# Expert units of a two-layer encoder: token rows fetched by an indirect transfer and turned on TensorE, and the last gated block turned inside the down product ahead of it

## The chip, the cores and the metric

The kernel runs on one core of a Trainium2 chip, as one program with one launch. The metric is the device time in microseconds (us) of an execution; lower is better.

## What is computed

The reference is an encoder trunk for 256 tokens of width 1024 in float32. Layer 0 is a neighbourhood attention beside a memory attention, and a dense SwiGLU. Layer 1 is a gated linear attention beside a memory attention, and a mixture of experts. Only the mixture matters here:

```python
def moe_swiglu(x, w_router, w_gate, w_up, w_down):   # x: the normalised tokens
    logits = xf @ w_router                           # 8 experts
    top_val, top_idx = lax.top_k(logits, 2)
    weights = jax.nn.softmax(top_val)
    # per expert e, for the tokens that chose it:
    #   y = (silu(x @ w_gate[e]) * (x @ w_up[e])) @ w_down[e]     w_gate, w_up 1024x3584, w_down 3584x1024
    # and h += weight * y for each token
```

Each expert holds 44 MB of weights, all eight are read once.

## The kernel before, in words

**Products in three parts.** Every weight block is split into a high part (rounded to the fast float32r type by ScalarE, `w_hi`) and a low part (the difference, by VectorE, `w_lo`), and so is the left operand. A product is then three matmuls, `w_hi*x_hi`, `w_lo*x_hi`, `w_hi*x_lo` (`mul3`, L1356 to L1360). A weight block of 128x2048 values (1 MB) is called a slot; three slots of `w_hi` and `w_lo` exist (CUT = 3), so the high part of slot j can be made only when TensorE has finished slot j-3 (`slot_done`). SyncE issues the loads, about ten slots ahead (`expert_loads`, L445 to L470), each one when the low part of the slot that lay in its place has been made.

**Units.** The mixture is worked off in units of up to 128 tokens of one expert. There are eight experts and up to three further units where an expert has more than 128 tokens; in the execution profiled there are eight units. All engines run the same loop over the units (`Fori`), each with its own body and semaphores between them. A unit has 42 slots: for c = 0 to 6 a gate product (2 slots), an up product (2 slots) and a down product (2 slots) over a block of 512 of the 3584 hidden columns. One slot is 12 matmuls with 512 columns.

**Order on TensorE in a unit** (L1884 to L1914): `hidden("gate", c)`, then `turn_hidden(c-1)` (four 128x128 transposes of the gated block of c-1, L1867), `hidden("up", c)`, `down(c-1)`. After c = 6: `turn_hidden(6)`, `gather(u+1, 0)`, `down(6)`, `gather(u+1, 1)`, and the scatter (L1911), eight matmuls. `gather(v, b)` (L1832 to L1838) forms half of the next unit's left operand, already turned: four output blocks of 128x128, each as two matmuls of `xn` (all 256 tokens) with the 0/1 matrix `pick` (256x128), which says which token stands in which place of the unit. The result is in PSUM bank 2+b; ScalarE copies it to `gx_hi` (`gather_high`, L744) and VectorE makes `gx_lo` (`gather_low`, L1258).

**Order on ScalarE** (L777 to L806): the high parts (L767), for each c silu (L787) and `hT_high(c-1)` (L780), and at the end of a unit the high part of slot 41, `hT_high(6)`, the high part of slot 42 (slot 0 of the next unit), `gather_high(u+1, 0)`, the high part of slot 43, the two halves of `y_hi` (L804) and `gather_high(u+1, 1)`.

**Order on VectorE** (L1320 to L1350): for each c the low parts (L1306) up to three slots ahead of the product, `hT_low(c-1)` (L1317), and after the low part of the slot three behind the up product the gated block `hid` (L1327), silu times up. `build_picks(u+1)` (L1255) follows `hid` of c = 5. At the end of a unit: the low part of slot 41, `hT_low(6)`, slot 42, `gather_low(u+1, 0)`, the two halves of `y_lo` (L1339), slot 43, `gather_low(u+1, 1)`, and two weighted additions to `h` (L1349). The low part of slot 44, the first of the next up product, comes after these.

**GpSimd** has only small operations, for the norms (`inverse_root`, L824 and L827) and in the linear attention (L845, L847), and nothing in the unit loop.

Of the kernel before, what the change touches and what calls it, by code (L numbers as in the profile page):

```python
# [18 lines left out]
ALU = mybir.AluOpType  # L19
ACT = mybir.ActivationFunctionType  # L20
F32 = mybir.dt.float32
F32R = mybir.dt.float32r
I32 = mybir.dt.int32
AX_X = mybir.AxisListType.X

# [103 lines left out]
def shape_constants(np):  # L129
# [7 lines left out]
    def put(name, a):  # L137
        full = np.zeros((P, a.shape[1]), np.float32)
        full[: a.shape[0]] = a
        col[name] = (sum(x.shape[1] for x in parts), a.shape[1])  # L140
        parts.append(full)
# [10 lines left out]
    put("ones", np.ones((P, P)))  # L152
    put("iota", np.broadcast_to(np.arange(P), (P, P)))
    x, dc = np.arange(SHIFT_W)[None, :], np.arange(RPB_C)[:, None]
    shifts = np.zeros((2, 2, 32, SHIFT_W), np.float32)
# [14 lines left out]
def build(nc, col, tables, shifts, x, mem, gains, rpb, gate_aug, g_norm, router, mem_kv, even_in, even_out,  # L170
          even_gate, even_up, even_down, odd_in, odd_out, exp_gate, exp_up, exp_down, out):
    with ExitStack() as ctx:
        def sb(name, shape, dt=F32):
            return ctx.enter_context(nc.sbuf_tensor(name, shape, dt))
# [28 lines left out]
        rt_lo = sb("rt_lo", [P, KD, E], F32R)  # L203
        unit_i = sb("unit_i", [P, 4], I32)
        states = sb("states", [P, 2, 3, DV])
        ARENA = 13464
# [68 lines left out]
        unit_f = take(4)  # L275
        r_at = top[0]
        gx_hi, gx_lo = xt_hi[:, :, 0:P], xt_lo[:, :, 0:P]
        y_hi, y_lo = xt_hi[:, :, P:T], xt_lo[:, :, P:T]
# [50 lines left out]
        def STATE_PS(d, k):  # L329
# [48 lines left out]
        y_half, y_hi_ready, y_lo_ready, scattered = (  # L378
            sem("y_half"), sem("y_hi_ready"), sem("y_lo_ready"), sem("scattered"))
        h_added = [sem(f"h_added_{t}") for t in range(TT)]  # L380

# [109 lines left out]
        def _(act):  # L491
# [262 lines left out]
            with act.Fori(0, n_more + E) as u:  # L754
# [28 lines left out]
                for c in range(NC):  # L783
# [6 lines left out]
                    if c == 4:  # L790
                        act.wait_ge(pick_turned, u + 1)
                        act.activation(pickT[:].rearrange("p t s -> p (t s)"), ps[:, 7, 0:2 * P],
                                       ACT.Copy).then_inc(pickT_ready, 1)
                high_unit(UNIT_SLOTS - 1)
                hT_high(NC - 1)
# [18 lines left out]
        def _(pool):  # L814
# [27 lines left out]
            for i in range(GH):  # L842
# [4 lines left out]
                pool.tensor_tensor(gss[:, 2, k], gss[:, 1, k], mhalf[:, 0:TT], ALU.pow).then_inc(o_rstd, 1)  # L847
            inverse_root(4, BY_HALF)
            inverse_root(5, BY_TOKEN)


        @block.vector
        def _(dve):
# [442 lines left out]
            with dve.Fori(0, n_more + E) as u:  # L1296
# [24 lines left out]
                for c in range(NC):  # L1321
                    if c >= 1:
                        low_unit(moe_slot("gate", c, 1) + CUT)
                        hT_low(c - 1)
                    unit_products(moe_slot("up", c, 1))
                    dve.wait_ge(silu_ready, u * NC + (c + 1))
                    dve.tensor_tensor(hid[:, c % 2, :], silu_sb[:, c % 2, :], ps[:, 2 * (c % 2) + 1, :],  # L1327
                                      ALU.mult).then_inc(hid_ready, 1)
                    if c == 5:
                        dve.wait_ge(pick_turned, u + 1)  # L1330
                        build_picks(u + 1)
                low_unit(UNIT_SLOTS - 1)
                hT_low(NC - 1)
# [21 lines left out]
        def _(pe):  # L1355
# [489 lines left out]
            with pe.Fori(0, n_more + E) as u:  # L1845
# [23 lines left out]

                def down(i):  # L1870
                    pe.wait_ge(hT_lo_ready, u * NC + (i + 1))
                    for half in range(2):
                        w = cut_slot(moe_slot("down", i, half), 2)
                        for n in range(2):
# [5 lines left out]
                            if i == NC - 1 and half == 1 and n == 0:  # L1880
                                ins.then_inc(y_half, 1)
                        ins.then_inc(slot_done, 1)

                for c in range(NC):  # L1884
# [10 lines left out]
                    hidden("up", c)  # L1895
                    if c >= 1:
                        down(c - 1)
                    if c == 3:
                        for t in range(TT):
                            ins = pe.transpose(ps[:, 7, P * t:P * (t + 1)], pick[:, t, :], ident)  # L1900
                        ins.then_inc(pick_turned, 1)
                turn_hidden(NC - 1)
                gather(u + 1, 0)
                down(NC - 1)
                gather(u + 1, 1)

# [50 lines left out]
```

## Time and profile before

| | |
|---|---|
| median of three runs | 1506.14 us (1502.95 to 1506.96) |
| the profiled execution: its own time | 1505.14 us |
| the profiled execution: span of the core | 1503.3 us |
| TensorE matmuls (PE) busy | 1457.3 us, 97% |
| TensorE weight loads (PEld) busy | 1240.3 us, 83% |
| VectorE (DVE) busy | 1170.6 us, 78% |
| ScalarE (ACT) busy | 978.4 us, 65% |
| GpSimd (POOL) busy | 21.4 us, 1% |
| DMA | 428.42 MB, mean 285 GB/s |
| mean granted TensorE clock | 0.985 of full speed |

The units fill the span from 499.3 us to the end. The profile gives for each group of instructions its busy time and what ended the idle time before it; the trace gives each instruction's start and duration. A matmul with 512 columns is shown with a duration of 0.39 us, but matmuls are pipelined: what counts is the distance from one start to the next. "PE" is the matmul, "PEld" the load of its stationary operand, which can run ahead of it. A float32 matmul of `gather` has two entries in the trace, so its eight matmuls are shown as x16; a transpose and a float32r matmul have one. The granted clock is given as a share of 2.4 GHz: 1.00 or 0.50.

### The profile page before, as it was taken

How to read it: one execution, taken by the hardware profiler on the slowest of the kernel's cores; microseconds unless marked ns; L12 is line 12 of the kernel's file. 1: busy time of each engine (PE TensorE's matmuls, PEld its weight loads, DVE VectorE, ACT ScalarE, POOL GpSimd, SP SyncE). 2: the span in 40 equal slices, each digit the busy share in tenths (PEclk: the TensorE clock that was granted, in tenths of full speed). 3: DMA queues.
4: the chain of work that ended last, by engine and by line, in shares of the span. 5: the costliest groups of instructions: out<-in, count | busy, mean ns of one | idle time of the engine just before them, and what ended most of it. 6: DMA issues, size and time to landing. Idle time of an engine off the chain costs nothing.

```text
span 1503.3 us, 20846 instructions
## 1 busy us (share of the span) xinstructions
PE 1457.3 (97%) x7832; PEld 1240.3 (83%) x7832; DVE 1170.6 (78%) x986; ACT 978.4 (65%) x904; POOL 21.4 (1%) x41
## 2 busy tenths in 40 slices
PE   6999999999998899999999999999999999999997
PEld 6986999998966788888888888888888888888885
DVE  5667544544774798898888888888888888898887
ACT  5455444334833677777777777777777777777775
POOL 1000000000010000000000000000000000000000
PEclk9999999999998999999999999999999999999999
DMA  9534555535535599899999989989989998998982
GB/s 320 192 115 137 186 194 183 181 115 162 161 113 196 183 387 369 317 376 376 324 344 385 376 302 383 374 310 372 378 308 369 383 365 312 375 369 319 372 323 90
DMA packets 198192, 428.42 MB, mean 285 GB/s; under 512 B 8805, under 2 KB 39041, under 8 KB 198146
## 3 DMA queue, kind: packets, MB, share of 16 engines
q1 hardware_dynamic: 198146, 427.79, 79.3%
q8 instruction: 30, 0.49, 0.1%
q14 instruction: 16, 0.13, 0.0%
HBM read 426.71 MB, written 1.05 MB: 285 GB/s over the span
## 4 chain that ended last, share of the span: by engine, by line
PE 88%; DVE 5%; ACT 3%; issue 2%; DMA 1%; POOL 0%; SPq 0%; DVEq 0%; POOLq 0%; ACTq 0%
PE ps L1358 27%; PE ps L1360 27%; PE ps L1359 27%; PE ps L1867 1%; DVE w_lo L1306 1%; PE ps L1836 1%; ACT w_hi L767 1%; PE ps L1911 1%; DVE w_lo L871 1%; ACT w_hi L505 1%; DMA raw<-mem_kv 1%; PE ps L1482 0%; PE ps L1804 0%; PE ps L1446 0%; PE ps L1379 0%
## 5 line engine op out<-in xcount | busy, mean ns | idle before, releaser
L1306 DVE TENSOR_TENSOR w_lo<-raw,w_hi 128x2048 fp32r<-128x2048 f32 (+1 forms) x224 | 442.4, 1984 | 61.5 <-ACT w_hi L767 60.7
L767 ACT ACTIVATE w_hi<-raw 128x2048 fp32r<-128x2048 f32 (+1 forms) x224 | 372.7, 1672 | 130.3 <-PE ps L1360 130.2
L1358 PE MATMUL ps<-w_hi,xt_hi 128*128 128x512 f32 (+2 forms) x1048 | 408.1, 389 | 3.0 <-DVE xt_lo L1193 1.5
L1360 PE MATMUL ps<-w_hi,xt_lo 128*128 128x512 f32 (+2 forms) x1048 | 400.9, 383 | 0.0
L1359 PE MATMUL ps<-w_lo,xt_hi 128*128 128x512 f32 (+2 forms) x1048 | 400.2, 382 | 0.0
L1306 DVE TENSOR_TENSOR w_lo<-arena,w_hi 128x2048 fp32r<-128x2048 f32 x144 | 295.6, 2053 | 29.8 <-ACT w_hi L767 29.1
L767 ACT ACTIVATE w_hi<-arena 128x2048 fp32r<-128x2048 f32 x144 | 248.6, 1727 | 82.6 <-PE ps L1360 82.3
L871 DVE TENSOR_TENSOR w_lo<-raw,w_hi 128x2048 fp32r<-128x2048 f32 (+2 forms) x69 | 149.5, 2170 | 124.2 <-ACT w_hi L505 124.1
L1358 PEld LDWEIGHTS ps<-w_hi,xt_hi 128*128 128x128 f32 x1048 | 197.3, 188 | 42.8 <-DVE w_lo L1306 3.3
L1360 PEld LDWEIGHTS ps<-w_hi,xt_lo 128*128 128x128 f32 x1048 | 197.4, 188 | 37.9
L1359 PEld LDWEIGHTS ps<-w_lo,xt_hi 128*128 128x128 f32 x1048 | 197.7, 189 | 34.7
L1358 PE MATMUL ps<-w_hi,hT_hi 128*128 128x512 f32 x560 | 219.1, 391 | 1.8 <-DVE hT_lo L1317 1.8
L1360 PE MATMUL ps<-w_hi,hT_lo 128*128 128x512 f32 x560 | 218.1, 389 | 0.0
L1359 PE MATMUL ps<-w_lo,hT_hi 128*128 128x512 f32 x560 | 218.0, 389 | 0.0
L505 ACT ACTIVATE w_hi<-raw 128x2048 fp32r<-128x2048 f32 (+2 forms) x69 | 125.4, 1818 | 118.3 <-PE ps L1360 109.7
L1358 PE MATMUL ps<-xt_hi,w_hi 128*128 128x256 f32 (+2 forms) x552 | 157.3, 285 | 1.3 <-DVE xt_lo L897 1.3
L1359 PE MATMUL ps<-xt_lo,w_hi 128*128 128x256 f32 (+2 forms) x552 | 156.7, 284 | 0.0
L1360 PE MATMUL ps<-xt_hi,w_lo 128*128 128x256 f32 (+2 forms) x552 | 156.6, 284 | 0.0
L1358 PEld LDWEIGHTS ps<-w_hi,hT_hi 128*128 128x128 f32 x560 | 105.2, 188 | 24.5 <-issue 3.3
L1360 PEld LDWEIGHTS ps<-w_hi,hT_lo 128*128 128x128 f32 x560 | 105.1, 188 | 22.1
L1359 PEld LDWEIGHTS ps<-w_lo,hT_hi 128*128 128x128 f32 x560 | 105.2, 188 | 21.2
L1358 PEld LDWEIGHTS ps<-xt_hi,w_hi 128*128 128x128 f32 (+2 forms) x552 | 103.7, 188 | 3.7 <-issue 3.1
(228 smaller groups left out, 1205.5 us busy)
## 6 DMA issues: line engine op xcount, KB each, us to landing
raw<-exp_gate SPq DMA_DIRECT2D x74, 1024.0 KB, 5.5
raw<-exp_up SPq DMA_DIRECT2D x48, 1024.0 KB, 5.6
arena<-exp_down SPq DMA_DIRECT2D x48, 1024.0 KB, 5.3
arena<-exp_up SPq DMA_DIRECT2D x40, 1024.0 KB, 7.0
raw<-exp_down SPq DMA_DIRECT2D x40, 1024.0 KB, 6.5
arena<-exp_gate SPq DMA_DIRECT2D x24, 1024.0 KB, 6.7
raw<-exp_up SPq DMA_DIRECT2D x32, 512.0 KB, 4.9
raw<-even_gate SPq DMA_DIRECT2D x11, 1024.0 KB, 5.4
```

The costliest lines, as they stand in the source:

```text
L505: act.activation(w_hi[:, n % CUT, 0:w], raw[:, n % RAW, 0:w], ACT.Copy).then_inc(hi_ready, 1)
L767: ins = act.activation(w_hi[:, n % CUT, at:at + src.shape[1]], src, ACT.Copy)
L871: dve.tensor_tensor(w_lo[:, n % CUT, 0:w], raw[:, n % RAW, 0:w], w_hi[:, n % CUT, 0:w].bitcast(F32), ALU.subtract).then_inc(lo_ready, 1)
L1306: ins = dve.tensor_tensor(w_lo[:, n % CUT, cols], src, w_hi[:, n % CUT, cols].bitcast(F32), ALU.subtract)
L1358: pe.matmul(dst, a[0], b[0], start=start, stop=False, skip_group_check=shared)
L1359: pe.matmul(dst, a[0], b[1], start=False, stop=False, skip_group_check=shared)
L1360: return pe.matmul(dst, a[1], b[0], start=False, stop=stop, skip_group_check=shared)
L1836: ins = pe.matmul(ps[:, 2 + b, P * (k % 4):P * (k % 4 + 1)], xn[:, t, P * k:P * (k + 1)], pick[:, t, :], start=(t == 0), stop=(t == 1))
L1867: ins = pe.transpose(ps[:, 4, P * j:P * (j + 1)], hid[:, i % 2, P * j:P * (j + 1)], ident)
L1911: ins = pe.matmul(ps[:, scatter_bank(t, n), :].rearrange("p (k t) -> p k t", k=4), pickT[:, t, :], y[:, 4 * n:4 * n + 4, :], start=(y is y ...
```

## The change

- After norm 4, GpSimd stores the normalised tokens `xn` to a DRAM tensor `xn_rows` (two transfers of 512 KB).
- In each unit, after `down(4)` (c = 5), TensorE multiplies `pick` with a column of token numbers, two float32 matmuls with one column each. VectorE copies the 128 numbers to `row_of`, after `hid` of c = 5. `build_picks` moves from c = 5 to c = 4.
- GpSimd, in a unit loop of its own, then makes a small addition, and an indirect transfer from `xn_rows` to `gx_rows`, one row of 4 KB for each of 128 partitions.
- The two calls of `gather(u+1, b)` in the loop become `turn_rows(u, b)`: a wait for the transfer and four transposes of 128x128. The gathers of unit 0 ahead of the loop stay.
- `turn_hidden(6)` moves from behind `down(5)` to between its two slots. ScalarE makes `hT_high(6)` ahead of the high part of slot 41, not behind it, and VectorE `hT_low(6)` ahead of the low part of slot 41.

```diff
@@ shape_constants
+    put("token", np.arange(P)[:, None] + P * np.arange(TT)[None, :])
@@ build
+        row_of = sb("row_of", [P, 1], U32)
+        xn_rows = nc.dram_tensor("xn_rows", (T, D), F32, kind="Internal").ap()
+        gx_rows = arena[:, r_at:r_at + D]
@@ ScalarE, unit loop
-                high_unit(UNIT_SLOTS - 1)
+                high_unit(UNIT_SLOTS - 2)
                 hT_high(NC - 1)
                 high_unit(moe_slot("down", NC - 2, 1) + CUT)
                 gather_high(u + 1, 0)
@@ GpSimd
             inverse_root(4, BY_HALF)
+            for t in range(TT):
+                pool.wait_ge(xn_ready, 16 + 2 * (t + 1))
+                nc.gpsimd.dma_start(xn_rows[P * t:P * (t + 1), :], xn[:, t, :]).then_inc(rows_kept, 16)
+            nc.gpsimd.memset(mhalf[:, 4:5], 0.0).then_inc(pool_turn, 1)
+            pool.wait_ge(units_ready, 1)
+            n_more = pool.value_load(unit_i[0:1, 0:1], min_val=0, max_val=3)
+            with pool.Fori(0, n_more + E) as u:
+                pool.wait_ge(rows_known, u + 1)
+                pool.tensor_tensor(mhalf[:, 4:5], mhalf[:, 0:1], mhalf[:, 1:2], ALU.add).then_inc(pool_turn, 1)
+                pool.wait_ge(rows_kept, 16 * TT)
+                nc.gpsimd.indirect_dma_start(gx_rows, None, xn_rows[:, :],
+                                             bass.IndirectOffsetOnAxis(ap=row_of[:, 0:1], axis=0)
+                                             ).then_inc(rows_in, 16)
@@ VectorE, unit loop
-                    if c == 5:
+                    if c == 4:
                         dve.wait_ge(pick_turned, u + 1)
                         build_picks(u + 1)
-                low_unit(UNIT_SLOTS - 1)
+                    if c == 5:
+                        dve.wait_ge(rows_counted, u + 1)
+                        dve.wait_ge(pool_turn, u + 1)
+                        dve.tensor_copy(row_of[:], ps[:, 7, 2 * P:2 * P + 1]).then_inc(rows_known, 1)
                 hT_low(NC - 1)
                 low_unit(moe_slot("down", NC - 2, 1) + CUT)
                 gather_low(u + 1, 0)
@@ TensorE, unit loop
-                def down(i):
+                def down(i, between=None):
                     pe.wait_ge(hT_lo_ready, u * NC + (i + 1))
                     for half in range(2):
+                        if half == 1 and between is not None:
+                            between()
                         w = cut_slot(moe_slot("down", i, half), 2)
...
+                def turn_rows(u, b):
+                    pe.wait_ge(rows_in, u * 16 + 16)
+                    for k in range(4 * b, 4 * b + 4):
+                        ins = pe.transpose(ps[:, 2 + b, P * (k % 4):P * (k % 4 + 1)], gx_rows[:, P * k:P * (k + 1)],
+                                           ident)
+                    ins.then_inc(gathered, 1)
...
                     hidden("up", c)
-                    if c >= 1:
+                    if c == NC - 1:
+                        down(NC - 2, between=lambda: turn_hidden(NC - 1))
+                    elif c >= 1:
                         down(c - 1)
...
+                    if c == 5:
+                        pe.wait_ge(pick_ready, u * 2 + 4)
+                        for t in range(TT):
+                            ins = pe.matmul(ps[:, 7, 2 * P:2 * P + 1], pick[:, t, :], const("token")[:, t:t + 1],
+                                            start=(t == 0), stop=(t == 1))
+                        ins.then_inc(rows_counted, 1)
-                turn_hidden(NC - 1)
-                gather(u + 1, 0)
+                turn_rows(u, 0)
                 down(NC - 1)
-                gather(u + 1, 1)
+                turn_rows(u, 1)
```

## Rows read from the trace of the kernel before

**Rows 1.** Busy time by engine, second unit (stretch, its length, PE ... PEclk, DMA share, GB/s)

```profile
624.30:747.00 122.70, 122.47 (x570) 101.47 (x569) 108.26 (x73) 91.72 (x71) 0.00 (x0) 1.00 0.98 359
```

**Rows 2.** Waits in 520 to 1480 us: us in total, times, longest

```profile
ACT w_hi L767 <- PE ps L1360: 220.8, 291, 2.2
...
PEld ps L1867 <- DVE arena L1327: 1.3, 7, 0.2
```

**Rows 3.** Timeline of PE, end of the first unit: start us, us, instruction

```profile
607.04 0.39 PE L1358 MATMUL ps<-w_hi,hT_hi 128*128 128x512 f32 x1
...
609.76 0.39 PE L1358 MATMUL ps<-w_hi,hT_hi 128*128 128x512 f32 x1
...
612.50 0.60 PE L1867 MATMUL ps<-cst,arena 128*128 128x128 f32 x4
612.93 1.95 PE L1836 MATMUL ps<-arena,xn 128*128 128x128 f32 x16
615.10 0.49 PE L1358 MATMUL ps<-w_hi,hT_hi 128*128 128x512 f32 x1 [0.22 <-DVE hT_lo L1317]
...
620.67 1.95 PE L1836 MATMUL ps<-arena,xn 128*128 128x128 f32 x16
622.37 0.47 PE L1911 MATMUL ps<-xt_hi,pickT 128*128 128x512 f32 x1
...
624.32 0.40 PE L1358 MATMUL ps<-w_hi,xt_hi 128*128 128x512 f32 x1
```

**Rows 4.** Timelines of ACT and DVE, same place: high and low part of slot 40, last gated block

```profile
607.25 1.92 ACT L767 ACTIVATE w_hi<-arena 128x2048 fp32r<-128x2048 f32 x1 [0.80 <-PE ps L1360]
...
609.20 2.29 DVE L1306 TENSOR_TENSOR w_lo<-arena,w_hi 128x2048 fp32r<-128x2048 f32 x1 [0.43 <-ACT w_hi L767]
611.41 0.68 DVE L1327 TENSOR_TENSOR arena<-arena,ps 128x512 f32<-128x512 f32 x1
```

**Rows 5.** Timelines of DVE and PEld: from second half of y_lo to slot 44

```profile
621.50 0.69 DVE L1339 TENSOR_TENSOR xt_lo<-ps,xt_hi 128x512 fp32r<-128x512 f32 x1 [0.23 <-ACT xt_hi L804]
...
627.29 4.48 DVE L1306 TENSOR_TENSOR w_lo<-raw,w_hi 128x2048 fp32r<-128x2048 f32 x2
...
629.62 0.19 PEld L1358 LDWEIGHTS ps<-w_hi,xt_hi 128*128 128x128 f32 x1
```

**Rows 6.** Timeline of PE: float32 products with eight columns (routing)

```profile
492.32 0.57 PE L1830 MATMUL ps<-arena,cst 128*128 128x8 f32 x2
...
492.74 0.57 PE L1829 MATMUL ps<-arena,cst 128*128 128x8 f32 x2
```

**Rows 7.** Timeline of PE: waits (in brackets) of the longest, a short one and the shortest that mattered

```profile
149.04 3.46 PE L1379 MATMUL ps<-cst,xn 128*128 128x128 f32 x16 [2.84 <-DVE xn L890]
...
431.05 1.22 PE L1751 MATMUL ps<-arena 64*96 64x192 f32 x12 [1.28 <-DVE states L1167]
...
452.41 0.72 PE L1358 MATMUL ps<-w_hi,xt_hi 128*128 128x512 f32 x1 [1.54 <-DVE xt_lo L1193]
```

**Rows 8.** Busy time and granted clock (third figure from the end) behind these waits

```profile
149.00:150.00 1.00, 0.96 (x5) 0.99 (x6) 0.55 (x1) 0.47 (x1) 0.91 (x1) 0.50 0.00 0
...
152.00:153.00 1.00, 0.50 (x4) 0.29 (x3) 0.83 (x2) 1.00 (x4) 0.00 (x0) 0.96 0.00 0
432.00:433.00 1.00, 0.92 (x8) 0.46 (x6) 0.85 (x4) 0.00 (x0) 0.00 (x0) 1.00 0.00 0
453.00:454.00 1.00, 1.00 (x4) 0.81 (x3) 0.00 (x0) 0.00 (x0) 0.00 (x0) 0.50 0.00 0
...
455.00:456.00 1.00, 1.00 (x4) 0.76 (x3) 0.00 (x0) 0.00 (x0) 0.00 (x0) 0.57 0.00 0
456.00:457.00 1.00, 1.00 (x7) 0.78 (x6) 0.00 (x0) 0.00 (x0) 0.00 (x0) 1.00 0.00 0
```

**Rows 9.** Timeline of DVE in the first unit: gated block of c = 5, what follows

```profile
594.59 0.68 DVE L1327 TENSOR_TENSOR arena<-arena,ps 128x512 f32<-128x512 f32 x1
...
595.58 4.69 DVE L1306 TENSOR_TENSOR w_lo<-raw,w_hi 128x2048 fp32r<-128x2048 f32 x3
```

**Rows 10.** Timelines of DVE and POOL: a GpSimd operation beside a low part, and alone

```profile
435.72 2.29 DVE L871 TENSOR_TENSOR w_lo<-raw,w_hi 128x2048 fp32r<-128x2048 f32 x1
...
435.88 2.18 POOL L845 TENSOR_SCALAR arena<-arena 128x2 f32<-128x2 f32 x1 [89.63 <-ACT arena L735]
...
440.13 0.19 POOL L845 TENSOR_SCALAR arena<-arena 128x2 f32<-128x2 f32 x1 [1.28 <-ACT arena L735]
```

**Rows 11.** Weight loads of the units, from issue to landing

```profile
DMA to landing us min/median/max: 3.2/5.5/13.3
```

More of the change, by code:

```diff
@@ L23 @@
 I32 = mybir.dt.int32
+U32 = mybir.dt.uint32
 AX_X = mybir.AxisListType.X
@@ L276, in build @@
         r_at = top[0]
+        gx_rows = arena[:, r_at:r_at + D]
+        assert r_at + D <= ARENA - ARENA_PLACES * HALF
         gx_hi, gx_lo = xt_hi[:, :, 0:P], xt_lo[:, :, 0:P]
@@ L379, in build @@
             sem("y_half"), sem("y_hi_ready"), sem("y_lo_ready"), sem("scattered"))
+        pool_turn, rows_kept, rows_counted, rows_known, rows_in = (
+            sem("pool_turn"), sem("rows_kept"), sem("rows_counted"), sem("rows_known"), sem("rows_in"))
         h_added = [sem(f"h_added_{t}") for t in range(TT)]
```

## The prediction

> **What bounds the kernel now.** I read the busy time by stretch first: in a unit of 122.70 us TensorE is busy 122.47 us at full clock, VectorE 108.26, ScalarE 91.72 [rows 1]. Then the waits: ScalarE waits for TensorE before 291 of its high parts, 220.8 us in all, and none of these waits ends with a load [rows 2]. So the units are bound by TensorE, and the DMA engines' share of 0.98 is no bound: the data lies ready. Last the timelines at the end of a unit, the only place that the change touches with more than small pieces. Call T the start of down(5), 607.04 us [rows 3]. TensorE's schedule from T is: down(5) in two slots of 2.72 us, four transposes at T+5.46 (0.43 us), the first gather at T+5.89, down(6) at T+8.06, second gather at T+13.63 (1.70 us), scatter at T+15.33, next gate product at T+17.28 [rows 3].
>
> **The first gather.** From its start to down(6) are 2.17 us, and the row of down(6) says that its last 0.22 us are a wait for the low part of the turned block [rows 3]. That gather costs TensorE 1.70 us, as the second one does, and covers the way of the gated block through ScalarE and VectorE. Four transposes cost 0.43. The swap takes out 2.17 - 0.43 = 1.74 us, and uncovers that way; the transposes of the gated block are moved ahead to cover it again. Can they be made there?
>
> **The moved transposes: when is the block ready?** They would start at T+2.72, at 609.76 [rows 3]. The gated block of c = 6 is not ready then. VectorE first makes the low part of slot 40, that needs its high part, and that needs the end of the up product, T. The rows: high part at T+0.21, 1.92 us; low part at T+2.16, 2.29 us; gated block at T+4.37, 0.68 us, ends at T+5.05 [rows 4]. Nothing in the change touches this chain: the high part starts when slot 37 ends, and the order on VectorE up to here is kept. Today the transposes come at T+5.46 and even so their operand load waits 1.3 us in seven units, about 0.2 us each [rows 2]. With a hop of 0.13 us (the block of the first wait above: low part to matmul) they start at T+5.18. TensorE stands still for 5.18 - 2.72 = 2.46 us, in each unit, with the second slot of down(5) queued behind it. Add 0.1 us for the restart of the 512-column matmuls after the transposes (a first matmul takes 0.49 us where others take 0.39 [rows 3]). Term: 2.46 + 0.1 - 1.74 = **+0.8 us** a unit. Behind it: the high part of slot 41 is now made after the turned block, at about T+6.3 to T+8.3, its low part by T+10.8 (0.6, 2 and 2.3 us pieces), and TensorE wants it at T+11.6. That fits.
>
> **The second gather.** It falls from 1.70 to 0.43 us. But VectorE's chain from the end of down(6) (620.67) is: second half of y_lo at 621.50, slot 43, gx_lo, two additions to h, and only at 627.29 the low part of slot 44, 2.24 us [rows 5]. TensorE loads slot 44's first operand at 629.62, 0.09 us after it is made [rows 5]. Nothing ahead of y_lo in this chain starts earlier, since y waits for down(6). So 1.27 us fewer on TensorE become a wait ahead of slot 44. I take -0.1 us, in seven units; the eighth ends in the same chain on VectorE and gets nothing.
>
> **The numbers of the rows.** Two float32 matmuls with `pick` as stationary operand. The nearest rows in form, with eight columns, stand 0.42 us apart [rows 6]; they ran at the half clock. The gathers' matmuls at full clock take 1.70/8 = 0.21 us each [rows 3]. So 0.42 to 0.84 us for two; nearer to the gathers' since the clock is full there: **+0.5 us** with a restart. VectorE waits for them: down(4) starts 4.37 us before its gated block, so at 590.22, ends at 595.66; the numbers are copied by about 596.5, while VectorE goes on at 595.58 today [rows 9]. The low part behind it, 2.25 us, is done at 598.8; TensorE wants it at 595.66 + 0.5 + 2.72 = 598.9. Nearly no room, and VectorE catches up over the next slots, where it idles some 0.3 to 0.4 us each. I take 0, and up to 0.3 a unit for the range.
>
> **GpSimd beside VectorE.** A GpSimd operation of 0.19 us took 2.18 us when it began behind a low part, and ended with it [rows 10]. So the addition and the transfer's read of `row_of` may each wait one low part; that hides. The other way about, VectorE held by GpSimd, no row shows: 0 to 0.5 us a unit, taken 0 because only the room at slot 35 is that small. The Trainium skill (SBUF — State Buffer, "Who interferes with whom") says that a VectorE instruction with two SBUF inputs and a GpSimd one that reads SBUF hold one port for the whole instruction, and the second blocks; every low part is such an instruction, and the trace agrees for GpSimd as the one held. By that rule VectorE could lose each GpSimd instruction's time once.
>
> **The transfer.** From 596.5 to the first use, 607.04 + 0.5 + 8.5 = 616.0, are 19.5 us. Two waits of 2.2 and the longest landing of a weight load, 13.3 us [rows 11], are 17.7. Hidden. Taken 0. The two stores of `xn` and the larger table come where loads are far ahead: 0, within 1 us.
>
> **What the standing still does to the clock.** From 140 us on the trace has four waits of TensorE between 1.54 and 2.84 us (the longest and the shortest stand here); behind each the granted clock went from 2.4 to 1.2 GHz. Behind the longest it was 0.50 from about 148.8 until 152.0; behind the shortest 0.50, 0.50 and 0.57 in three successive us [rows 7, 8]. A wait of 1.28 us left it at 1.00 [rows 7, 8]. The new wait is 2.46 us, with transposes behind it. TensorE is the bound there, so 3.2 us at half speed cost 1.6 us. I take the fall in seven units of eight, as four of four fell but one may be missed: 7 x 1.6 = **+11.2 us**. Bounds: 0 (never) and 8 x 1.7 = 13.6.
>
> **Sum.** 8 x (0.8 + 0.5) - 7 x 0.1 + 11.2 = 20.9 us. On the profiled execution's own time, 1505.14, that is 1526.0; its span is 1.8 us less, and the median of the runs 1.0 us more. I forecast 1526.5.
>
> **Rivals.**
> (a) The wait is there but the clock holds, or falls in few units: 9.7 us or some more, 1515 to 1519. For it: the units are denser in matmuls than most places where it fell. Against: nothing in the rows held it behind more than 1.28 us. Chance 0.22.
> (b) Faster. The block is ready at the half-way point, so that the transposes cost no wait. It decides at T+2.72: if the gated block ends before, the terms are -1.74 + 0.1 + 0.5 - 0.1 a unit, -10 us, 1496. For it: the design needs it. Against: the chain of three rows has no slack, its high part cannot start before T. Chance 0.07.
> (c) No change to speak of: the second gather's 1.27 us count fully, since VectorE's chain gives way by 1 us, and the clock holds: 8 x 1.3 - 7 x 1.2 = +2 us, 1508. Against: the load at 0.09 us behind the low part. Chance 0.06.
> (d) The indirect transfer lands late, or holds VectorE up again and again. From 19.5 us on each us counts in eight units: 25 us would be +44 on top, near 1565. For it: no row shows such a transfer, beside DMA engines that are at 0.98. Chance 0.08. The Trainium skill (DMA: Bandwidth & Descriptors, "Anatomy of one DMA") gives 2.0 us and the bytes over 436 GB/s for a GpSimd transfer, by estimate 3.2 us for 512 KB; no run here shows it.
> The forecast keeps 0.57.
>
> **How the numbers follow.** About 0.3% (4.5 us) is what a measurement of this kernel can tell. Faster is (b), 0.07; same is (c) and the foot of (b), 0.07; slower the rest, 0.86. The range: below, rival (a) from its sum less the small bounds (the numbers at 0.42), 1512; above, all eight falls and 0.7 us a unit from VectorE's side (slot 35, GpSimd), 1535. It leaves out (b), (c), (d) and little more, some 0.2.
>
> **What would show it.** Right: between the two slots of down(5) a wait of PE on L1327 of about 2.4 us in eight units; a granted clock of 0.50 for some 3 us behind it; down(6) ending 14.4 us after T plus the clock's 1.6 instead of 13.6; a new wait of PE of up to 1 us on a low part ahead of slot 44; the unit 2.8 us longer. Wrong: no such wait (then (b)), the clock at 1.00 (a), a wait on the transfer ahead of the rows' transposes (d), or VectorE's idle time behind L1327 of c = 5 growing beyond 1 us.

## The result and the profile after

The changed kernel took 1525.21 us, median of 4 runs (1522.58 to 1528.13), the kernel before 1504.64 us (median of 4, 1502.95 to 1506.96; of the first three it was 1506.14): a ratio of 1.013 with a 95% interval of 1.0113 to 1.0147. It is slower by 20.6 us. The forecast was 1526.5. The profiled execution took 1527.01 us with a span of 1525.0, 21.7 us longer than that of before.

The page's totals for the changed kernel, and its chain of the work that ended last. TensorE's products (L1382 to L1384) are 78% of that chain:

```profile
PE 1456.0 (95%) x7672; PEld 1230.9 (81%) x7672; DVE 1172.7 (77%) x994; ACT 978.9 (64%) x904; POOL 54.7 (4%) x60
...
PE ps L1382 26%; PE ps L1384 26%; PE ps L1383 26%; ACT w_hi L775 2%; PE ps L1891 2%; DVE w_lo L1327 1%; PE ps L1951 1%; DVE h L1373 1%; DVE w_lo L892 1%; ACT w_hi L513 1%; DMA raw<-mem_kv 1%; PE ps L1828 1%; PE ps L1506 0%; PE ps L1470 0%; PE ps L1775 0%
```

The waits between 520 and 1500 us (us in all, times, longest). The last gated block is made on L1348 now, and its transposes are L1891:

```profile
...
ACT w_hi L775 <- PE ps L1384: 226.5, 298, 1.8
...
PEld ps L1891 <- DVE arena L1348: 21.1, 8, 2.6
PE ps L1891 <- DVE arena L1348: 17.7, 8, 2.2
DVE hT_lo L1338 <- ACT hT_hi L788: 10.6, 7, 1.8
PEld ps L1382 <- DVE w_lo L1327: 7.6, 7, 1.1
DVE row_of L1356 <- PE ps L1940: 7.5, 8, 0.9
...
PE ps L1382 <- DVE w_lo L1327: 4.7, 7, 0.7
```

Read it against [rows 2]. There the operand load of these transposes waited 1.3 us in all and the matmuls behind it do not appear. Now TensorE itself waits 17.7 us, eight times 2.2 us: once in each unit. A second wait that was not there has 4.7 us in seven places: the low part of slot 44, ahead of the next unit. No wait on the indirect transfer appears anywhere. The largest wait in these lines is still ScalarE's on TensorE; only GpSimd's for the row numbers is longer (970.4 us). TensorE is the bound, and neither wait holds it up.

TensorE at the end of the first unit, the place of [rows 3]. T, the start of down(5), is 610.47 here; the two slots of down(5) are to either side of L1891, the rows' transposes are L1913, the scatter is L1951:

```profile
610.47 0.39 PE L1382 MATMUL ps<-w_hi,hT_hi 128*128 128x512 f32 x1
...
612.96 0.39 PE L1384 MATMUL ps<-w_hi,hT_lo 128*128 128x512 f32 x1
615.56 0.66 PE L1891 MATMUL ps<-cst,arena 128*128 128x128 f32 x4 [2.22 <-DVE arena L1348]
615.98 0.52 PE L1382 MATMUL ps<-w_hi,hT_hi 128*128 128x512 f32 x1
616.29 0.63 PE L1383 MATMUL ps<-w_lo,hT_hi 128*128 128x512 f32 x1
616.72 0.63 PE L1384 MATMUL ps<-w_hi,hT_lo 128*128 128x512 f32 x1
...
620.39 0.60 PE L1913 MATMUL ps<-cst,arena 128*128 128x128 f32 x4
620.75 0.48 PE L1382 MATMUL ps<-w_hi,hT_hi 128*128 128x512 f32 x1
...
626.33 0.60 PE L1913 MATMUL ps<-cst,arena 128*128 128x128 f32 x4
627.07 0.47 PE L1951 MATMUL ps<-xt_hi,pickT 128*128 128x512 f32 x1
...
629.00 0.40 PE L1382 MATMUL ps<-w_hi,xt_hi 128*128 128x512 f32 x1
...
635.28 0.50 PE L1382 MATMUL ps<-w_hi,xt_hi 128*128 128x512 f32 x1 [0.64 <-DVE w_lo L1327]
```

From T to the next gate product are 18.53 us (629.00 - 610.47); they were 17.28. The gathers are gone, and the stretch is longer all the same. Both reasons are in the rows: 2.22 us of standing still at 615.56, and behind it 512-column matmuls that start 0.43 us apart (616.29, 616.72) where twelve of them take 2.72 us, 0.23 each, at the full clock [rows 3]. The granted clock (third figure from the end) says the same. What stands behind its column is the DMA engines' share and GB/s:

```profile
614.00:615.00 1.00, 0.00 (x0) 0.00 (x0) 1.00 (x2) 0.00 (x0) 0.00 (x0) 1.00 1.06 391
...
617.00:618.00 1.00, 1.00 (x4) 0.71 (x3) 0.58 (x1) 1.00 (x2) 0.00 (x0) 0.50 1.02 377
618.00:619.00 1.00, 1.00 (x4) 0.81 (x3) 0.22 (x1) 0.74 (x1) 0.00 (x0) 0.50 1.07 403
...
620.00:621.00 1.00, 1.00 (x8) 0.86 (x7) 1.00 (x2) 0.41 (x1) 0.00 (x0) 1.00 0.94 363
```

TensorE's clock is at 2.4 GHz during the wait, at 1.2 GHz in 617 to 619, and back at 2.4 GHz in 620. The same stretch in two other units, TensorE alone (length, busy, clock, DMA share, GB/s), one with the fall and the only one without:

```profile
970.00:1005.00 35.00, 32.78 (x146) 0.95 0.96 344
1096.00:1131.00 35.00, 32.78 (x152) 1.00 0.93 348
```

VectorE shows why TensorE stands still. It is the chain of [rows 4], 3.4 us later, as T is:

```profile
612.62 2.29 DVE L1327 TENSOR_TENSOR w_lo<-arena,w_hi 128x2048 fp32r<-128x2048 f32 x1 [0.43 <-ACT w_hi L775]
614.83 0.68 DVE L1348 TENSOR_TENSOR arena<-arena,ps 128x512 f32<-128x512 f32 x1
```

The up product that the block needs ended at T. VectorE takes the low part of slot 40 first, and that one waits for ScalarE's high part; the block ends 5.04 us behind T, and TensorE wants it 2.7 us behind T.

**Where the 21.7 us of the span went.** The transposes of the last block begin in eight units; from the first to the eighth are 884.35 us (615.56 to 1499.91), so 126.34 a unit against 124.04 before. Six of these seven periods are 126.5 to 126.6 long and the one behind the unit without a fall 124.96: a fall costs 1.6 us, and the rest of the change 0.92 a unit. But the units began late too. The routing's products stand ahead of all of them, and ahead of everything that the change adds but the two stores of `xn`. Before and after:

```profile
491.45 0.59 PE L1826 MATMUL ps<-arena,cst 128*128 128x8 f32 x2 [2.82 <-DVE arena L1231]
```

```profile
494.09 0.59 PE L1850 MATMUL ps<-arena,cst 128*128 128x8 f32 x2 [2.82 <-DVE arena L1252]
```

These 2.6 us are not the change's. filled_wait, below, has the same program as the changed kernel up to this row and beyond, and there the row begins at 490.18; in all the kernels below it lies between 489.59 and 494.14. Part of the difference can be seen in the granted clock ahead of the row. Between 440 and 460 us, before and after:

```profile
440.00:460.00 20.00, 16.64 (x80) 11.81 (x81) 10.10 (x28) 3.08 (x12) 2.65 (x6) 0.83 0.13 47
```

```profile
440.00:460.00 20.00, 16.38 (x88) 10.92 (x86) 10.32 (x30) 3.60 (x15) 2.66 (x6) 0.74 0.16 52
```

The clock averages 0.83 in one and 0.74 in the other. A wait of TensorE near its start ends 0.9 us later in the changed kernel (442.74 against 441.82), and the same wait behind it 2.3 us later (480.96 against 478.70). So each profile is read from this routing row to its end: 1011.85 us before, 1030.91 after, **+19.06 us**.

The column "from routing" below is that reading for every kernel. The period is the mean of seven units, from the last block's transposes of the first unit to those of the eighth. The median is of all timed executions. The ratio is to the kernel before as timed in the same group: it had 1506.32 us (13 runs) beside the first four and 1505.07 (12 runs) beside the last four.

The last column counts the units in which the clock fell in the one profiled execution; the other executions of a kernel have no such count.

| kernel | median us (range, runs) | ratio, 95% | from routing | period | falls in units |
|---|---|---|---|---|---|
| before | | | 0 | 124.04 | 0 |
| after | 1525.21 (1522.58 to 1528.13, 4) | 1.013 (1.0113 to 1.0147) | +19.1 | 126.34 | 7 |
| hid_first | 1494.97 (1492.65 to 1497.97, 4) | 0.9926 (0.9909 to 0.9943) | -11.6 | 122.55 | 0 |
| filled_wait | 1515.95 (1511.67 to 1517.45, 4) | 1.0062 (1.0045 to 1.0079) | +7.7 | 124.98 | 0 |
| turn_late | 1509.48 (1506.21 to 1512.2, 10) | 1.0019 (1.0008 to 1.003) | +2.8 | 124.37 | 0 |
| move_only | 1525.46 (1524.49 to 1529.23, 4) | 1.013 (1.0113 to 1.0147) | +18.8 | 126.45 | 2 |
| move_hid_first | 1501.12 (1499.57 to 1502.98, 8) | 0.9974 (0.9963 to 0.9984) | -3.6 | 123.52 | 0 |
| rows_unused | 1511.61 (1509.34 to 1514.21, 5) | 1.0047 (1.0033 to 1.0061) | +3.9 | 124.52 | 0 |
| half_filled | 1514.05 (1511.96 to 1515.99, 5) | 1.0058 (1.0044 to 1.0072) | +8.0 | 124.97 | 0 |
| adds_late | 1491.55 (1491.13 to 1494.84, 5) | 0.9921 (0.9907 to 0.9934) | -14.1 | 122.02 | 0 |

### The profile page after: what moved, and what is told of

The parts are those of the page before. It is cut to its first block, busy times and chain, and to the rows that moved or that the text cites. A ratio compares the mean times of both kernels' runs of the same rounds, so it can differ in the third digit from the quotient of the medians.

```text
span 1525.0 us, 20597 instructions
## 1 busy us (share of the span) xinstructions
PE 1456.0 (95%) x7672; PEld 1230.9 (81%) x7672; DVE 1172.7 (77%) x994; ACT 978.9 (64%) x904; POOL 54.7 (4%) x60
## 4 chain that ended last, share of the span: by engine, by line
PE 86%; DVE 6%; ACT 4%; issue 3%; DMA 1%; POOL 0%; DVEq 0%; SPq 0%; POOLq 0%; ACTq 0%
PE ps L1382 26%; PE ps L1384 26%; PE ps L1383 26%; ACT w_hi L775 2%; PE ps L1891 2%; DVE w_lo L1327 1%; PE ps L1951 1%; DVE h L1373 1%; DVE w_lo L892 1%; ACT w_hi L513 1%; DMA raw<-mem_kv 1%; PE ps L1828 1%; PE ps L1506 0%; PE ps L1470 0%; PE ps L1775 0%
## 5 line engine op out<-in xcount | busy, mean ns | idle before, releaser
L1382 PE MATMUL ps<-w_hi,xt_hi 128*128 128x512 f32 (+2 forms) x1048 | 408.4, 390 | 7.8 <-DVE w_lo L1327 5.7
L1384 PE MATMUL ps<-w_hi,xt_lo 128*128 128x512 f32 (+2 forms) x1048 | 400.5, 382 | 0.0
L1382 PEld LDWEIGHTS ps<-w_hi,xt_hi 128*128 128x128 f32 x1048 | 197.0, 188 | 47.5 <-DVE w_lo L1327 9.1
L1384 PEld LDWEIGHTS ps<-w_hi,xt_lo 128*128 128x128 f32 x1048 | 196.9, 188 | 38.1
L1382 PE MATMUL ps<-w_hi,hT_hi 128*128 128x512 f32 x560 | 224.1, 400 | 0.0
L1383 PE MATMUL ps<-w_lo,hT_hi 128*128 128x512 f32 x560 | 222.2, 397 | 0.0
L1384 PE MATMUL ps<-w_hi,hT_lo 128*128 128x512 f32 x560 | 221.9, 396 | 0.0
L1382 PE MATMUL ps<-xt_hi,w_hi 128*128 128x256 f32 (+2 forms) x552 | 157.8, 286 | 1.4 <-DVE xt_lo L918 1.4
L1384 PE MATMUL ps<-xt_hi,w_lo 128*128 128x256 f32 (+2 forms) x552 | 157.0, 284 | 0.0
L1384 PEld LDWEIGHTS ps<-w_hi,hT_lo 128*128 128x128 f32 x560 | 107.7, 192 | 23.1
L1382 PEld LDWEIGHTS ps<-w_hi,hT_hi 128*128 128x128 f32 x560 | 108.1, 193 | 21.8
L1383 PEld LDWEIGHTS ps<-w_lo,hT_hi 128*128 128x128 f32 x560 | 107.7, 192 | 21.7
L1382 PEld LDWEIGHTS ps<-xt_hi,w_hi 128*128 128x128 f32 (+2 forms) x552 | 104.3, 189 | 3.6 <-issue 3.2
```

Of the source, the lines that this page charges most:

```text
L1382: pe.matmul(dst, a[0], b[0], start=start, stop=False, skip_group_check=shared)
L1383: pe.matmul(dst, a[0], b[1], start=False, stop=False, skip_group_check=shared)
L1384: return pe.matmul(dst, a[1], b[0], start=False, stop=stop, skip_group_check=shared)
```

## The experiments

**hid_first: the block ahead of slot 40.** If the order of two instructions on VectorE is what makes TensorE wait, then reversing it in the changed kernel takes the wait and the falls away. `unit_products` makes the low parts up to slot 40's and then waits for the product; now the low parts go up to the slot before it, and slot 40's follows the block.

```diff
@@ VectorE, unit loop, last c only
-                    unit_products(moe_slot("up", c, 1))
+                    low_unit(moe_slot("up", c, 1) + CUT - 1)
+                    dve.wait_ge(slot_done, u * UNIT_SLOTS + (S_MOE + moe_slot("up", c, 1) + 1))
                     dve.wait_ge(silu_ready, u * NC + (c + 1))
                     dve.tensor_tensor(hid[:, c % 2, :], silu_sb[:, c % 2, :], ps[:, 2 * (c % 2) + 1, :],
                                       ALU.mult).then_inc(hid_ready, 1)
+                    low_unit(moe_slot("up", c, 1) + CUT)
```

> The changed kernel with one order reversed on VectorE: the gated block of c = 6 is made ahead of the low part of slot 40, not behind it. My theory (the cost of the change is TensorE's wait for this block at the half of down(5), and the fall of the clock behind it): the block then ends about 0.9 us after T, ahead of T+2.72 where TensorE wants it, so both the 2.2 us wait and the falls vanish; down(6) starts at about T+6.4 where the kernel before had T+8.06. Per unit -1.6 + 0.5 for the row numbers - 0.1 at the second gather, in eight units -10: about 1495 us, faster than both kernels, clock 1.00 through all units. Rival 1 (the tail is set by something behind the block, such as the low part of slot 41 or the transfer): a wait of the same size turns up elsewhere, 1515 to 1525. Rival 2 (only the clock mattered): 1514.

It took 1494.97 us, ratio 0.9926 (0.9909 to 0.9943): faster than both. VectorE and TensorE in the first unit, where T is 606.42:

```profile
605.86 2.29 DVE L1327 TENSOR_TENSOR w_lo<-arena,w_hi 128x2048 fp32r<-128x2048 f32 x1 [0.32 <-ACT w_hi L775]
608.06 0.68 DVE L1352 TENSOR_TENSOR arena<-arena,ps 128x512 f32<-128x512 f32 x1
608.66 2.28 DVE L1327 TENSOR_TENSOR w_lo<-arena,w_hi 128x2048 fp32r<-128x2048 f32 x1
```

```profile
609.15 0.60 PE L1897 MATMUL ps<-cst,arena 128*128 128x128 f32 x4
609.50 0.48 PE L1388 MATMUL ps<-w_hi,hT_hi 128*128 128x512 f32 x1
...
612.34 0.60 PE L1919 MATMUL ps<-cst,arena 128*128 128x128 f32 x4
```

The block ends 2.3 us behind T, not the 0.9 that were expected: VectorE has to finish the low part of slot 39 first (605.86, 2.29 us). That is still ahead of T + 2.72, and the transposes start at T + 2.73 with nothing in brackets: there is no wait. Slot 40's low part is made right behind it, without waiting, and is early enough. The period falls from 126.34 to 122.55 us. One order on one engine is worth 30 us in this kernel (both medians), and the change as a whole is a gain only with it.

**turn_late: the transposes back behind down(5).** The changed kernel with the moved part alone undone: the four transposes stand ahead of the rows' as they stood ahead of the first gather, and ScalarE's and VectorE's orders are as before (their lines are left out below).

```diff
-                    if c == NC - 1:
-                        down(NC - 2, between=lambda: turn_hidden(NC - 1))
-                    elif c >= 1:
+                    if c >= 1:
                         down(c - 1)
...
+                turn_hidden(NC - 1)
                 turn_rows(u, 0)
```

> The changed kernel with the last gated block turned where the kernel before turned it, behind down(5), with ScalarE's and VectorE's orders set back too; the rows still come by the indirect transfer. My theory: down(6) starts at T+8.06 as before, because there the first gather only covered the way of the block through ScalarE and VectorE; TensorE waits about 1.5 us instead of gathering. So the row part gives nothing there: 0.5 for the numbers, -0.1 at the second gather, +3 us in all, 1508 us if the clock holds; with a fall of the clock in half or more of the units (a wait of 1.54 us had one behind it) 1514 to 1521. Rival (the saved gather counts fully): 1.3 us less in each unit, about 1497.

It took 1509.48 us in 10 runs, ratio 1.0019 (1.0008 to 1.003). TensorE again, T at 605.60:

```profile
611.05 0.60 PE L1892 MATMUL ps<-cst,arena 128*128 128x128 f32 x4
611.48 0.60 PE L1914 MATMUL ps<-cst,arena 128*128 128x128 f32 x4
613.66 0.49 PE L1383 MATMUL ps<-w_hi,hT_hi 128*128 128x512 f32 x1 [1.58 <-DVE hT_lo L1338]
```

From the rows' transposes to down(6) are 2.18 us. With the gather there they were 2.17 [rows 3]. Everything that the swap saved at this place came back as a wait, 1.58 us where it was 0.22, since the turned block needs the same time for its way through ScalarE and VectorE. The gather had covered that way. This is why the change had to move the transposes, and the clock stayed at 1.00 in all units behind these eight waits of 1.6 us.

**move_only: the move without the swap.** The kernel before with the transposes between the halves of down(5), and its gathers kept (the edit is turn_late's, the other way about).

> The kernel before with only the second part of the change: the last gated block turned between the slots of down(5), with the new orders on ScalarE and VectorE; the gathers stay, no row numbers, no transfer. My theory: the wait of 2.2 us plus 0.1 for the restart is paid, and 0.4 us of waiting ahead of down(6) vanish, +2.0 us a unit = +16, and 11 for seven falls of the clock: 1531 us. Rival (the cost of the change lies in the row part, GpSimd and the transfer): within 5 us of 1505.

1525.46 us, ratio 1.013 (1.0113 to 1.0147), against 1531 expected. The wait is as forecast, `PE` on the block 17.7 us in 8 times. The falls are not. Two units beside each other (stretch, length, PE busy, clock, DMA share, GB/s), and the transposes in both:

```profile
590.00:625.00 35.00, 32.79 (x152) 0.95 0.91 323
717.00:752.00 35.00, 32.79 (x163) 1.00 0.91 334
```

```profile
612.67 0.66 PE L1866 MATMUL ps<-cst,arena 128*128 128x128 f32 x4 [2.21 <-DVE arena L1327]
740.19 0.66 PE L1866 MATMUL ps<-cst,arena 128*128 128x128 f32 x4 [2.21 <-DVE arena L1327]
```

Six of eight stretches show 1.00, two 0.95. So a wait of 2.21 or 2.22 us brings the clock down in some units and not in others, with the same instructions around it. The period is 126.0 us without a fall and 127.5 with one; the move alone, without any fall, costs 2.0 us a unit.

**filled_wait and half_filled: TensorE kept busy in the wait.** To price the falls apart from the wait, the changed kernel gets matmuls of 512 columns ahead of the moved transposes, nine and four of them. They are added work: they write a PSUM bank whose contents have been read by then, and nothing reads what they leave. The diff is filled_wait's; half_filled has 4 for 9.

```diff
+                        def filled():
+                            for _ in range(9):
+                                pe.matmul(ps[:, 7, :], hT_hi[:, 1, 0:P], hT_hi[:, 1, :], start=True, stop=True)
+                            turn_hidden(NC - 1)
-                        down(NC - 2, between=lambda: turn_hidden(NC - 1))
+                        down(NC - 2, between=filled)
```

> The changed kernel with nine matmuls of 512 columns added on TensorE ahead of the moved transposes, into a PSUM bank that nobody reads; they take 9 x 0.227 = 2.0 us and fill the 2.2 us wait for the gated block, which stays. My theory (clock term of 1.6 us in seven of eight units on top of the wait): the clock stays at 1.00, the wait is as long as before, filled: about 1525 - 11 = 1514 us. Rival (the clock does not depend on this wait, or the wait was longer than it had to be because of the clock): 1522 to 1526, or clearly under 1512.

> The changed kernel with four matmuls of 512 columns (0.9 us) in the wait at the half of down(5), into a bank that nobody reads; 1.3 us of waiting stay. A wait of 1.28 us had no fall of the clock behind it in the kernel before, and one of 1.6 us none in the run with the late turn: the clock holds, 1515 to 1516 as with nine matmuls. Rival (every wait of this place has falls behind it, whatever its length): 1520 or more.

They took 1515.95 and 1514.05 us, ratios 1.0062 (1.0045 to 1.0079) and 1.0058 (1.0044 to 1.0072). With nine:

```profile
736.27 0.66 PE L1891 MATMUL ps<-cst,arena 128*128 128x128 f32 x4 [0.17 <-DVE arena L1348]
```

With four:

```profile
615.59 0.66 PE L1891 MATMUL ps<-cst,arena 128*128 128x128 f32 x4 [1.31 <-DVE arena L1348]
```

The transposes come at T + 5.10 in either (VectorE decides that), the clock is at 1.00 in all units of both, and the periods are 124.98 and 124.97 us. That is the period that the changed kernel itself shows in its one unit without a fall, 124.96. So the changed kernel's time has two parts: 11.1 us of falls (19.1 - 8.0, from routing) that idle matmuls take away, and some 8 us that they don't. Useless work made this kernel some 10 us faster. It is no remedy; hid_first is.

**move_hid_first: both orders, without the swap.** What is the swap worth once the block is early? The kernel before with the move and with hid_first's order, gathers kept.

> The kernel before with the last gated block turned between the slots of down(5) and, on VectorE, made ahead of the low part of slot 40; the gathers stay and there is no row part. My theory: no wait at the half of down(5), and the 0.4 us of waiting ahead of down(6) vanish, nothing else: 2.72 + 0.43 + 0.1 + 2.72 + 1.70 = T+7.67 for down(6) where it was T+8.06; -0.3 to -0.4 us in each of eight units, 1502 to 1503.5 where the kernel before has 1506. So of the 11 us that the early block gives in the kernel with the rows (1495), about 8 need the rows' transposes in the gathers' place. Rival (the early block alone gives it): 1497 or less.

1501.12 us in 8 runs, ratio 0.9974 (0.9963 to 0.9984). Its period is 123.52 us, 0.52 less than before, and hid_first's is 0.97 less than this one. So with the block early, the rows by transfer are worth 8.0 us from the routing on (-11.6 against -3.6).

They are worth as much with the block late, once the transposes are moved. The periods of the units without a fall, gathers against rows:

| last block's transposes | gathers | rows | rows less gathers |
|---|---|---|---|
| behind down(5) | 124.04 (before) | 124.37 (turn_late) | +0.33 |
| between its slots, block late | 126.02 (move_only) | 124.96 (after) | -1.06 |
| between its slots, block early | 123.52 (move_hid_first) | 122.55 (hid_first) | -0.97 |

What decides whether the swap pays is the place of the transposes. The order on VectorE decides whether the move pays: with the gathers it costs 2.0 us a unit with the block late and gains 0.5 with it early, with the rows it costs 0.6 and gains 1.8.

**rows_unused: the transfer without its use.** turn_late with the two gathers on TensorE kept in place of the rows' transposes. The numbers, the copy, GpSimd's addition and the transfer all run, TensorE waits for the transfer, and what it brought is not read.

```diff
                 def turn_rows(u, b):
                     pe.wait_ge(rows_in, u * 16 + 16)
-                    for k in range(4 * b, 4 * b + 4):
-                        ins = pe.transpose(ps[:, 2 + b, ...], gx_rows[...], ident)
-                    ins.then_inc(gathered, 1)
+                    gather(u + 1, b)
```

> The changed kernel with the last gated block turned late, as before, and with the gathers doing the work: the row numbers, GpSimd's addition and the indirect transfer run and TensorE waits for the transfer, but its rows are not used. This is the price of the row part alone. My theory: 0.5 us a unit for the two matmuls of the numbers, all else hidden: +4 us over the kernel before, 1510. Rival (GpSimd and the transfer hold VectorE or the loads up): more than 8 us over.

1511.61 us, ratio 1.0047 (1.0033 to 1.0061). From the routing on it is 3.9 us above the kernel before, where 4 were expected for the numbers; its period is 0.48 us longer, and its list of TensorE's waits is that of the kernel before, none of them new. The medians stand 6.5 us apart. Of what is more than 3.9, 1.15 us lie ahead of the routing in the two profiles (492.60 against 491.45); the rest lies between executions. So the transfer and GpSimd's part cost TensorE nothing that shows in a period beyond the 0.48 us, which is what two matmuls were priced at.

**adds_late: the next wait.** hid_first still waits ahead of slot 44, in the units' change: its waits have the same `4.7, 7, 0.7` there. If VectorE's additions to `h`, 2.47 us, are what keeps the low part of slot 44 back, then that low part ahead of them, with its high part ahead of the next unit on ScalarE, takes the wait away. The low part below was the first of the next unit; the loop behind it holds the additions. After the last unit there is one load and one low part more than before.

```diff
@@ VectorE, end of the unit (ScalarE's order is changed in the same way)
                 gather_low(u + 1, 1)
+                low_unit(UNIT_SLOTS - 1 + CUT)
                 for t in range(TT):
...
```

> The kernel with the early gated block, and on VectorE the low part of slot 44 (the first of the next unit's up product) ahead of the two additions to h, not behind them; ScalarE makes its high part at the end of the unit body, and the loads after the last unit are three slots, not two. My theory of the second gather (what it gives is lost to VectorE's chain, 0.7 us of waiting ahead of slot 44): the wait ahead of slot 44 vanishes, but the low part of slot 45 is then 0.4 to 0.8 us late, so -0.3 us in seven units; at the end one low part more stands ahead of the last additions, +2.2: 1494 to 1497, no change to the kernel with the early block alone. Rival (the chain gives way): -0.7 in seven units +2.2, 1492.

1491.55 us, ratio 0.9921 (0.9907 to 0.9934). The waits of this kernel:

```profile
PEld ps L1399 <- DVE w_lo L1338: 4.0, 7, 0.6
PE ps L1399 <- DVE w_lo L1338: 0.6, 4, 0.2
```

The wait is down from 4.7 us to 0.6 and the period from 122.55 to 122.02. The gain of 0.53 us a unit is plain in the trace; the intervals of the two ratios overlap, so as whole kernels they are not told apart. The gain lies between the 0.3 that was expected and the rival's 0.7. From the routing on the two kernels are 2.5 us apart (-14.1 against -11.6); seven times 0.53 are 3.7, so the low part more at the end cost some 1.2 us, not the 2.2 expected. Its median, 0.8% under the kernel before, is the lowest of this study.

## Why the prediction was right

**The wait.** The argument was that three rows of VectorE's and ScalarE's chain end at T + 5.05 and that nothing in the change touches them, so that transposes wanted at T + 2.72 come at T + 5.18. They came at T + 5.09 (615.56 - 610.47) with the block done at T + 5.04. The forecast start was 0.09 us too late, in all eight units. This is the step on which the sign hung, and hid_first shows that it is the cause: the one order reversed, the wait is gone.

**The first gather.** The rows' transposes take 0.36 us of TensorE (620.39 to 620.75) where 2.17 stood, so the swap took out 1.81 us and not 1.74. From T to the end of down(6) the after has 15.86 us (626.33 - 610.47) for 13.63 [rows 3]; less the fall's 1.6 that is +0.63 where +0.8 stood.

**The second gather.** It was priced at -0.1 us though it is 1.27 us shorter, since VectorE's chain ends later. The chain is the same length to the hundredth of a microsecond: from the end of down(6) to the low part of slot 44 are 6.62 us in both (627.29 - 620.67 [rows 5], and 632.95 - 626.33). TensorE takes up slot 44 8.95 us behind the end of down(6) (635.28 - 626.33) where it took 9.11 before (629.78), a gain of 0.16, and the wait of 0.64 us ahead of it is new. adds_late is the experiment on this step: with the chain shortened, 0.53 us a unit come out.

**The numbers.** +0.5 was taken from rows at the half clock and at the full one; rows_unused has a period 0.48 us longer, with nothing else new in TensorE's waits. The worry about VectorE at slot 35 was justified in form only. VectorE waits 0.94 us for the numbers in each unit, then makes the same low parts, of two slots in three instructions:

```profile
599.12 0.16 DVE L1356 CAST row_of<-ps 128x1 uint32<-128x1 f32 x1 [0.94 <-PE ps L1940]
599.22 4.56 DVE L1327 TENSOR_TENSOR w_lo<-raw,w_hi 128x2048 fp32r<-128x2048 f32 x3
```

No wait of TensorE on slot 35 came of it, so the 0 was right and the 0.3 of the range not needed.

**GpSimd and the transfer.** In the first unit:

```profile
599.37 2.20 POOL L865 TENSOR_TENSOR mhalf<-mhalf 128x1 f32<-128x1 f32 x1 [114.94 <-DVE row_of L1356]
601.74 1.82 POOL L867 DMA_INDIRECT arena<-xn_rows,row_of  x1 [0.17 <-issue]
```

An addition of one element a partition takes 2.20 us, as long as the low part beside it: it began 0.15 us behind the first of the three instructions, one of 2.29 us, and ended 0.06 us behind it. That is the behaviour of [rows 10], where another small operation had 0.19 us alone; this one never ran alone in a unit. VectorE's three instructions took 4.56 us beside it, 4.69 without it [rows 9]; VectorE was not seen to lose anything. The Trainium skill (SBUF — State Buffer, "Who interferes with whom") lets whichever comes second block; the trace shows that for GpSimd, and no row shows it for VectorE, where GpSimd came second each time. The eight transfers of L867, from issue to landing:

```profile
DMA to landing us min/median/max: 7.5/8.3/9.2
```

Issued at 601.74, such a transfer is there before 611, and its first use is at 620.39. Rival (d) had a margin of over 9 us against it. The estimate by the Trainium skill (DMA: Bandwidth & Descriptors, "Anatomy of one DMA") was 3.2 us; the measured landing is more than twice that, beside DMA engines whose share was 0.94 from 601 to 611 us, and the measurement decides. What share the other traffic has in it was not tested. Nothing hung on it.

**The falls.** Seven were forecast because four of four waits from 1.54 us up had brought one, and seven came, 1.6 us each: 126.6 us against 124.96. The size of one is shown three times over, by the unit without it and by both filled kernels. The number seven was luck. The profile of before has in fact five such waits (those at 441.82 and 478.70 us are of 2.08 and 2.21), each with a fall, so the reading was low by one; but what one profile shows of a wait isn't what the next one shows. This is the wait of 1.54 us of [rows 7] in the changed kernel, and the clock behind it:

```profile
456.21 0.47 PE L1382 MATMUL ps<-w_hi,xt_hi 128*128 128x512 f32 x1 [1.54 <-DVE xt_lo L1214]
```

```profile
457.00:458.00 1.00, 1.00 (x6) 0.82 (x5) 0.00 (x0) 0.00 (x0) 0.00 (x0) 1.00 0.00 0
```

No fall, where [rows 8] have one. Of the ten profiles of this study, whose programs are alike at this place, six have a fall behind this wait and four have none (after, hid_first, half_filled, move_hid_first); in hid_first the wait of 2.08 us ahead of it has none either. move_only has the new wait of 2.21 us and two falls in eight, and turn_late's waits of 1.58 us brought none. So the reasoning on this term had the price right, while the count came out without its reason being sound. Had after behaved as move_only did, it would have been 8 us faster (5 x 1.6), at rival (a)'s 1515 to 1519. That rival's 0.22 was if anything small. Only one of after's four executions was profiled, the one of 1527.01 us with a mean clock of 0.976; the two fastest (1522.58 and 1523.41) have 0.982, and may have had fewer falls in the units or ahead of them.

**The sum.** 8 x (0.8 + 0.5) - 0.7 + 11.2 = 20.9 us was forecast. From the routing on +19.1 were measured: 7 x 1.6 for the falls and 8 x 1.0 for the rest, where the sum had 1.2 (9.7 in all). The 1.0 is 0.63 for the first gather and 0.48 for the numbers less 0.16 for the second gather, within 0.05. The difference between the medians is 20.6. The profiled execution's 2.6 us from ahead of the routing were in no step of the sum; after and filled_wait, whose programs are the same up to that row, have it 3.9 us apart (494.09 and 490.18). Two figures beside the sum are off: rival (a)'s 9.7 us less the small bounds on 1505.14 give 1514, not 1512, and 44 us on top of the forecast are 1570, not 1565. Neither bears on the result.

## What to carry to other kernels

Work that is taken off the bound engine is a gain only where no other chain was running under it: here the first gather covered a chain through two other engines, and the second one ended ahead of a chain that stayed as long. When a dependent step is moved earlier, follow its producer back on every engine, and look at what each of them does just before it; the thing in the way may be one instruction that nobody needs yet. Compare two profiles from a common instruction behind the unrelated stages, since these alone can differ by some microseconds. And don't take a count of clock falls from a single profile.

## What the runs showed of the hardware

**The same wait does not always bring the clock down.** Behind waits of TensorE of 2.21 to 2.22 us the granted clock fell from 2.4 to 1.2 GHz in seven units of eight of one kernel and in two of eight of another, whose units differ in how the next unit's tokens are gathered. Behind sixteen waits of 1.58 us and 1.31 us (turn_late, half_filled) it never fell; behind one of 1.54 us earlier in the kernel it fell in six of ten profiles. The fall doesn't keep to the end of the wait either: in the seven units of after it began between 0.2 us ahead of it and 0.9 us behind it. What sets it apart stays open. It is not the DMA traffic alone: in move_only a stretch with the fall and one without both have a DMA share of 0.91.

**Added matmuls that nobody reads paid for themselves.** Four of them took 0.91 us out of the wait (2.22 to 1.31 us), and the clock stayed at 1.00 in eight of eight units of the one profile; the kernel's median is 11 us under the changed kernel's.

**A GpSimd operation that began behind a low part ended with it.** One element a partition took 2.20 us at L865 in each of eight units; two elements a partition took 0.19 us with no low part beside them [rows 10]. It matters when a transfer is queued behind such an operation: here 4.4 us pass from the start of the copy to `row_of` (599.12) to the end of the transfer's issue (601.74 + 1.82).
